# A two-layer diffusion backbone block on one core: 16x16 blocks of the triangular solve inverted on VectorE, another order at the transitions, and the first shift vectors as rows

## What is computed

```
def modulate(h, shift, scale):
    return h * (1.0 + scale) + shift
...
mod = s_lat @ w_ada[l] + b_ada[l]            # s_lat = silu(c); the context has its own vector
...
A = jnp.where(tril_strict, beta[..., :, None] * kk * decay_mat, 0.0)
lhs = A + jnp.eye(C, dtype=F32)
rhs = jnp.concatenate([v * beta[..., None], k * (beta * jnp.exp(G))[..., None]], axis=-1)
sol = lax.linalg.triangular_solve(lhs, rhs, left_side=True, lower=True, unit_diagonal=True)
```

## Time and profile before

| | before |
|---|---|
| median of 3 runs | 2459.61 us (2457.1 to 2466.61) |
| the profiled execution | 2457.2 us, its span 2455.5 us |
| busy, TensorE / VectorE / ScalarE / GpSimd | 2357.0 / 1384.5 / 872.4 / 217.9 us |
| granted clock of TensorE, mean | 0.989 |

### The profile page before, as it was taken

How to read it: one execution, slowest core, us unless ns; L and a number is a source line. 1 busy time by engine, 2 the same in 40 slices (tenths; PEclk the granted TensorE clock), 3 DMA queues, 4 the chain that set the end, 5 groups by cost and what they waited for, 6 DMA issues and landing times. The chain is left out here.

```text
span 2455.5 us, 36528 instructions
## 1 busy us (share of the span) xinstructions
PE 2357.0 (96%) x14022; PEld 2012.8 (82%) x14022; DVE 1384.5 (56%) x2315; ACT 872.4 (36%) x1343; POOL 217.9 (9%) x280
## 2 busy tenths in 40 slices
PE   5999999999999999999999999999999989998998
PEld 5788878886569796888888888888898689888998
DVE  3777875724553435578885255554464543456554
ACT  1533322533441214353322253332255431245553
POOL 3001122000000000211001100000200001001001
PEclk9999999999999999999999999999999999999999
DMA  6455553322020204356554334444334211134555
GB/s 245 134 191 188 192 173 114 130 86 78 32 67 19 78 1 139 115 168 200 188 198 123 95 116 151 148 145 123 94 122 134 65 54 30 47 119 148 182 175 147
DMA packets 96461, 304.05 MB, mean 124 GB/s; under 512 B 10593, under 2 KB 17249, under 8 KB 95329
## 3 DMA queue, kind: packets, MB, share of 16 engines
q1 hardware_dynamic: 76912, 230.87, 29.2%
q0 software_dynamic: 18720, 69.21, 8.6%
q10 hardware_dynamic: 720, 2.44, 0.3%
HBM read 291.99 MB, written 10.49 MB: 123 GB/s over the span
## 5 line engine op out<-in xcount | busy, mean ns | idle before, releaser
L1799 PE MATMUL ps<-h_hi,w_hi 128*128 128x512 f32 (+1 forms) x2176 | 779.5, 358 | 37.2 <-DVE w_lo L1276 26.5
L1801 PE MATMUL ps<-h_hi,w_lo 128*128 128x512 f32 (+1 forms) x2176 | 760.3, 349 | 0.0
L1800 PE MATMUL ps<-h_lo,w_hi 128*128 128x512 f32 (+1 forms) x2176 | 760.2, 349 | 0.0
L1276 DVE TENSOR_TENSOR w_lo<-raw,w_hi 128x1024 fp32r<-128x1024 f32 (+2 forms) x416 | 475.3, 1146 | 470.2 <-ACT w_hi L709 465.9
L709 ACT ACTIVATE w_hi<-raw 128x1024 fp32r<-128x1024 f32 (+2 forms) x416 | 405.2, 975 | 621.7 <-DMA raw<-in_w_down 316.1
L1799 PEld LDWEIGHTS ps<-h_hi,w_hi 128*128 128x128 f32 x2176 | 418.2, 192 | 127.2 <-issue 41.9
L1801 PEld LDWEIGHTS ps<-h_hi,w_lo 128*128 128x128 f32 x2176 | 418.0, 192 | 51.6
L1800 PEld LDWEIGHTS ps<-h_lo,w_hi 128*128 128x128 f32 x2176 | 418.7, 192 | 48.6
L1799 PE MATMUL ps<-a_hi,w_hi 128*128 128x512 f32 (+1 forms) x1050 | 363.0, 346 | 8.3 <-DVE buf_b L1699 3.4
L1801 PE MATMUL ps<-a_hi,w_lo 128*128 128x512 f32 (+1 forms) x1050 | 360.4, 343 | 0.0
L1800 PE MATMUL ps<-a_lo,w_hi 128*128 128x512 f32 (+1 forms) x1050 | 359.0, 342 | 0.0
(11 more groups left out here) (230 smaller groups left out, 1966.5 us busy)
## 6 DMA issues: line engine op xcount, KB each, us to landing
raw<-in_w_up SPq DMA_DIRECT2D x176, 512.0 KB, 3.8
ada<-in_w_ada_t POOLq DMA_DIRECT2D x128, 512.0 KB, 3.9
raw<-in_w_down SPq DMA_DIRECT2D x64, 384.0 KB, 3.2
raw<-in_w_gate SPq DMA_DIRECT2D x48, 512.0 KB, 3.7
raw<-in_w_down SPq DMA_DIRECT2D x64, 320.0 KB, 2.9
raw<-in_w_proj SPq DMA_DIRECT2D x32, 512.0 KB, 3.6
raw<-in_w_merge SPq DMA_DIRECT2D x16, 512.0 KB, 3.9
raw<-in_w_out SPq DMA_DIRECT2D x16, 512.0 KB, 3.5
```

The costliest lines, as they stand in the source:

```text
L1276: vec.tensor_tensor(w_lo[:, j % RING, 0:cols], raw[:, j, 0:cols], w_hi[:, j % RING, 0:cols].bitcast(F32), ALU.subtract).then_inc(s_lo, 1)
L1799: pe.matmul(out, wh, rows_hi[:, i, c], start=first, stop=False)
L1800: pe.matmul(out, wh, rows_lo[:, i, c], start=False, stop=False)
L1801: return pe.matmul(out, wl, rows_hi[:, i, c], start=False, stop=last)
```

## The change

LEVELS begins at 16. `sub_blocks` on VectorE inverts the 16x16 diagonal blocks: it gathers them by 32x32 transposes out of amT into xm, folds the two directions into one triangle, inverts by forward substitution in 28 linked steps, masks, and writes by transposes into tm, which GpSimd has zeroed. Both directions' starting values lie in tm; `t_mat` and `u_mat` name which buffer is T and which U. One set of sixteen transposes gives the other buffer. The prep points get 3 units in place of 4, the Gram products come before the first prep gates, and the lowers of the last finished gate blocks move into the levels. In `split_norm` casts and lowers 0 and 1 come at k = 1 and 3 and the root at k = 7; lag is 3. The first shift vectors are made as rows, [2 x 1024], by 16 matmuls with the conditioning vectors as stationary operand, ahead of the sums; ScalarE copies them out and eight small transposes bring them to columns. w_ada's first part is laid out to suit.

```
-LEVELS = (2, 4, 8, 16, 32, 64)
+LEVELS = (16, 32, 64)
+SUB = LEVELS[0]
+QUAD = 2 * SUB
+PREP_UNITS = 3
...
-        units += [4] * PREP_POINTS + [n - 4 * PREP_POINTS] + list(SCAN_UNITS[l])
+        units += [PREP_UNITS] * PREP_POINTS + [n - PREP_UNITS * PREP_POINTS] + list(SCAN_UNITS[l])
...
-                    for d in range(2):
-                        same = um[:, 8 * d:8 * d + 8, :].rearrange("p q (i c) -> p q i c", c=2)[:, :, :, d]
...
-                    last.then_inc(uid.sem, 1)
+                    pool.memset(tm[:, :, :], 0.0).then_inc(zro.sem, 1)
...
                 if s == 0:
+                    act.wait_ge(s_adad, 1)
+                    act.activation(ada_rows[0:2, :, :], ps[0:2, 2:4, :], ACT.Copy).then_inc(s_adr, 1)
                     casts(0, 2)
...
-                    if k == 2:
+                    if k == 1:
                         weights(0)
+                    if k == 3:
+                        weights(1)
                     if k == 4:
                         last_square(1)
-                        weights(1)
-                    if k == 6:
+                    if k == KD - 1:
                         root(1)
...
+                def sub_blocks(w):
+                    for q in range(P // QUAD):
+                        r = slice(q * QUAD, (q + 1) * QUAD)
+                        last = vec.transpose(sub_raw[r, :].rearrange("p (i t h) -> p i t h", t=16, h=2),
+                                             amT[r, :, r].rearrange("p t (h i) -> p i t h", h=2))
+                    link(last)
...
+                    link(vec.tensor_scalar(sums, raws[:, :, 0, :], half_minus(0), None, ALU.mult))
+                    link(vec.scalar_tensor_tensor(sums, raws[:, :, 1, :], half_minus(1), sums, ALU.mult, ALU.add))
+                    link(vec.tensor_tensor(t, sums, sub_sum.rearrange("p (i j) -> p j i", i=SUB), ALU.add))
+                    link(vec.tensor_copy(sub_t[:, 0:SUB * SUB:SUB + 1], ones[:, 0:SUB]))
+                    for j in range(1, SUB - 1):
+                        size = [P, SUB - 1 - j, j]
+                        part = sub_sum[:, 0:size[1] * j].rearrange("p (i c) -> p i c", c=j)
+                        link(vec.tensor_tensor(part, t[:, j + 1:SUB, j:j + 1].to_broadcast(size),
+                                               t[:, j:j + 1, 0:j].to_broadcast(size), ALU.mult))
+                        link(vec.tensor_tensor(t[:, j + 1:SUB, 0:j], t[:, j + 1:SUB, 0:j], part, ALU.add))
...
+                    vec.wait_ge(edn.sem, edn.at(l, 4 * w + 4))
+                    sub_blocks(w)
...
+                        for n in late[2 * i:2 * i + 1]:
+                            lower(n % RING, b0 + n)
...
-                        if i < 4 and (l == 0 or i % 2 == 0):
-                            decay_queries(w, i)
+                        for n in late[2 * i + 1:2 * i + 2]:
+                            lower(n % RING, b0 + n)
+                        for j in ((0, 1), (2, 3), ())[i]:
+                            if l == 0 or j % 2 == 0:
+                                decay_queries(w, j)
...
+            def first_shifts():
+                pe.wait_ge(s_cact, 1)
                 for k in range(KD):
+                    if k % (ADA_FIRST // 4) == 0:
+                        pe.wait_ge(s_first[k // (ADA_FIRST // 4)], 16)
+                    for m in range(2):
+                        ins = pe.matmul(ps[0:2, 2 + m, :], c_act[:, k, :], ada_first[:, k, m * TOK:(m + 1) * TOK],
+                                        start=(k == 0), stop=(k == KD - 1))
...
-                lag = 2
+                lag = 3
...
-                        if p == 0 and k == 4:
+                        if p == 0 and k == 5:
                             part_sums(s, 1)
...
+                    pe.wait_ge(low.sem, low.at(l, w + 1))
...
+                            elif d:
+                                for j in range(2):
+                                    for q in range(8):
+                                        ins = pe.transpose(ps[:, 2 + 2 * j + q // 4, (q % 4) * P:(q % 4 + 1) * P],
+                                                           tm[:, 8 * j + q, :], ident)
+                                    ins.then_inc(tr0.sem, 1)
+                                pe.wait_ge(tr0e.sem, tr0e.at(l, 2 * w + 2))
+                            columns(i, d)
```

More of the change, by code:

```diff
@@ L1602, in mixer_vec @@
                     gates(delta_point(l, w, PREP_POINTS))
+                    vec.wait_ge(edn.sem, edn.at(l, 4 * w + 4))
+                    sub_blocks(w)
+                    late = [GATE_BLOCK + g + 3 for g in gates_finished(l, delta_point(l, w, PREP_POINTS))]
+                    assert len(late) <= 3
                     for i, b in enumerate(LEVELS):
@@ L2135, in mixer_pe, with columns @@
                     pe.wait_ge(rowd.sem, rowd.at(l, 4 * w + 4))
-                    for d in range(2):
-                        pe.wait_ge(u1.sem, u1.at(l, 2 * w + d + 1))
+                    pe.wait_ge(low.sem, low.at(l, w + 1))
+                    def columns(i, d):
+                        b = LEVELS[i]
                         for q in range(8):
-                            ins = pe.transpose(ps[:, 2 + 2 * d + q // 4, (q % 4) * P:(q % 4 + 1) * P],
-                                               um[:, 8 * d + q, :], ident)
-                        ins.then_inc(tr0.sem, 1)
+                            t = t_mat(d)[:, q, :].rearrange("p (i c) -> p i c", c=2 * b)[:, :, b * d:b * (d + 1)]
+                            ins = pe.matmul(ps[:, d, q * HD:(q + 1) * HD].rearrange("p (i c) -> p i c", c=b),
+                                            amT[:, 8 * d + q, :], t, start=True, stop=True)
+                        ins.then_inc(xps.sem, 1)
@@ L2316, in constants @@
     c[:, C_TRI + P:C_TRI + 2 * P] = i[:, None] >= i[None, :]
-    c[even, C_M1 + even + 1] = -1.0
-    c[even + 1, C_M1 + P + even] = -1.0
+    for h in range(2):
+        c[:, C_HALF + h] = -1.0 * (i % 2 == h)
+    s = np.arange(SUB)
+    low = (i[:, None, None, None] % 2 == np.arange(2)[None, None, :, None]) & (s[None, None, None, :] >= s[None, :, None, None])
+    c[:, C_LOW:C_HALF] = low.reshape(P, -1)
     c[:, C_MIN:C_MIN + P] = np.where(i[:, None] <= i[None, :], 0.0, NEVER)
@@ L2357, in lay_out @@
     out["cT"] = np.stack([v["c"][0], v["c_ctx"]], 1).reshape(KD, P, 2).transpose(1, 0, 2)
-    out["w_ada"] = blocks(v["w_ada"][0][:, :KD * P])
+    out["w_ada"] = v["w_ada"][0][:, :KD * P].reshape(KD, P, KD * P)
     out["w_ada_t"] = v["w_ada"].transpose(0, 2, 1).reshape(DEPTH * ADA, P, D)[KD:]
```

133 lines of the change are left out of this document (67 added, 66 removed).

## The result

The changed kernel takes 2401.98 us in the median of four runs (2394.06 to 2405.19), the kernel before 2460.75 (2457.1 to 2466.61): ratio 0.9745, 95% interval 0.9717 to 0.9774, so it is faster: by 59 us between the medians, by some 63 by the ratio (56 to 70 with its interval). The experiments' gains against the kernel before go by their ratios. The forecast was 2354 and its range ended at 2386: right sign, but a gain of 105 us was forecast and 63 came. Ratios are of executions in the usual state, and one of run 6's four (3713.43 us, at a granted clock of 0.553) is left out of them.

What follows compares the result with a forecast made beforehand. The prediction took TensorE, busy 2357.0 us or 96% of the span, as the bound. Gains of 80 (solve), 13 (transitions) and 12 (start), 105 us in all, from 2457.2 gave 2352, stated as 2354, range 2337 to 2386.

Steps and rivals of the forecast that it cites:

- Levels removed, 107.8 us: Triangular solve: levels 2, 4 and 8 go, 8.98 us each in four solves, 107.8 us off TensorE, all counting.
- I charge 2.5 twice: 5 us: Solves of layer 1: TensorE idles some 12 us and restarts at a low clock, charged 2.5 us twice.
- Rival B: Clock stays low in the start's shift products (15 us lost) and all four solve restarts (5 us): 2374 us; chance 0.10.
- I take 0.70 each: VectorE's block in the solve: eight transposes at 0.70 us, 5.6 in all, within a block of 14.4 us.
- rival D: Solve's strided transposes move element by element; at 5 us each the kernel is slower, 2492 us; chance 0.03.
- VectorE's arrival: Solve: VectorE is ready to start its block 23.9 us after the stage's start in layer 0.
- The order after the wait: Solve's first level: first L2161 comes 6.9 us after the wait, against 5.8 before; delay called 1.2 us with a hop.
- The transitions, 13 us: Four transitions: earlier casts and lowers shorten TensorE's waits for w_lo; 13 us booked, bounds 3 and 17.
- With idle pieces under 2 us I expect it high: Transitions: TensorE's clock stays high, gaining 4.8 us where it had stayed at 0.66.
- Rival C: Transitions give nothing, as the late h_lo takes the place of w_lo: 2364 us; chance 0.10.
- The start, 12 us: Start: 16 products of 512 columns replace 64 small ones for the first shifts, ending at 41 us; gain 12 us.
- A: VectorE's block in the solve is dearer, 20 us, with transposes at twice the price: 2376 us; chance 0.16.

Runs made afterwards that it cites:

- run 6: Changed kernel with the block's eight strided 32-partition transposes replaced by gathering copies and two transposes of 128 partitions: 2397.56 us.
- run 4: Changed kernel with unneeded identity products ahead of TensorE's wait for the blocks, 30 in layer 0 and 70 in layer 1: 2395.5 us.
- run 7: Changed kernel with 33 and 66 unneeded products ahead of the block waits and six in the gap inside the first level: 2377.63 us.
- run 10: Changed kernel again without an edit, for a second profile: median 2401.21 us.
- run 5: Changed kernel with nine more dependent VectorE instructions behind the last block, to price transposes and views: one execution, 2391.9 us.
- run 12: run 11 with 4, 5 and 7 unneeded products ahead of the three waits of each transition: 2360.59 us.
- run 2: Kernel before with the change to the four transitions alone: ratio 0.9959, 10 us faster.
- run 11: run 8 with five more unneeded products ahead of the last solve's wait: 2359.08 us.
- run 9: Kernel before with 21 unneeded dependent VectorE passes in layer 0 ahead of the solve's last starting matrix, making TensorE wait: 2494.68 us.
- run 8: Changed kernel with 128-partition block transposes, unneeded products ahead of block waits (20 and 56), in the gap (six) and in the start: 2366.06 us.

## Why the prediction was wrong

It missed by 41.6 us against the profiled execution, and by 48 against the median. Of the 41.6, 34.2 are the solves', 4.8 the transitions', 1.9 the start's and 0.7 the rest's. By its own steps:

- **Levels removed, 107.8 us**: right. Of the three levels left in each solve the second takes 8.97 us at full clock (756.62 to 765.59), as each of the six did before; the first takes 12.19 with what moved into it, which the sum had as a delay.
- **"I charge 2.5 twice: 5 us"**: this step failed, and it is the largest, 16.6 us in the profiled execution (21.6 less 5) and 21.7 in the second profile. The clock was charged for the long waits of layer 1 alone; for layer 0, with a wait that I put at 2 us, nothing was booked. Runs 4, 6 and 7 show that this is wrong twice over. The stretch behind a wait of 4.3 us loses no less than the one behind 13.6, and the gap of 1.15 us inside the first level, which the change itself brings (the copies that direction 1 waits for), brings the clock down in three of four solves where the wait is filled (14.4 us). Where the gap is filled too, 1.6 us are lost in one solve, behind the 1.79 us of wait that were left, and nothing in the others. Wait and gap together cost 2.5 to 9.8 us in each solve. Rival B named the cause and its sign, but priced it at 2.5 per solve too, by the one row that had it, and put 15 of its 20 us in the start, where they were not lost. The Trainium skill, TensorE: Matmul & The Clock Gate, Part 1, warns that a kernel's slow products differ in number from run to run, and run 10 bears that out; it calls this under 1% of a typical span and advises against fitting it. Here 21.6 to 26.7 us are 0.9 to 1.1% of the span, but the largest part of what is missing from a gain of 4%.
- **"I take 0.70 each"**: the transposes were mis-sized, 1.05; with the closing pass, 1.01, the blocks take 17.8 to 18.0 us and not 14.4, 13.9 in all four. (The terms of the sum came to 14.6; 14.4 was used.) The bounds (11.5 to 20) held it, and both halves of the argument have something in them: 0.70 is the price of a transpose (run 5), and strides do make it dearer, by half and not by the factor of seven that rival D wanted. The row that I used against D, passes through strided views of tm, spoke of views with runs of 2 to 64 neighbours. The small steps (6.6 against 6.7) were right.
- **VectorE's arrival**: it began the block 24.6 and 24.9 us after a stage's start in layer 0 (23.9 forecast) and 20.9 and 19.1 in layer 1 (18.5). With what else is left in the solves this makes 3.7 us.
- **The order after the wait** ("6.9 us", then the rest): right. At full clock the first level takes 12.19 us; the prediction's terms make 12.26 (6.9 to the update's products, then what a level of 8.98 has behind its first 3.62), and ScalarE's copy is waited for as forecast.
- **The transitions, 13 us**: 8.2, within the bounds of 3 to 17. The waits are 0.35, 0.89 and 1.43 us in the first, 2.67 in all where 1.7 were forecast and 4.34 stood before. "With idle pieces under 2 us I expect it high" failed: the clock was 0.90 in three and 0.82 in the second, which lost all it had gained. Run 12 shows that the gaps have to do with it: with them filled it is 1.00 in all four. But in the fourth transition of run 2 and the first of run 11 it was 1.00 with the gaps unfilled (15.2 us each), so the gaps don't bring it down every time. Rival C did not come true.
- **The start, 12 us**: 12.3 at the first product, by a path that was faster than thought (the shifts ended at 38.0 and not 41) into a later wait. 2 us were lost by the first transition, to a longer wait for h_lo (2.13 us and not 1.13 and 0.27) and a second stretch at the low clock (0.62 over 66 to 70 us). These 1.9 us are the start's part of the miss.
- **The rivals and the range.** A (the block at 20) and B (clock) were each priced alone, at 2376 and 2374; both came true in part at once, B in the solves. The range took in A with C, but not A with B.

## What to carry to other kernels

A wait that a change puts on TensorE costs more than its length: here 2.4 and 6.7 us of clock behind a wait alone (run 9), 2.5 to 9.8 with a gap of 1.1 us behind it, and no less behind a wait of 4 us than behind one of 14. So four new waits cost 69 us with their clock (46.9 and 21.6) against the 108 that the removed levels brought. Price it like that from the start, look for the gaps of about 1 us as well (run 4's three cost 14.4 us), and if the wait can't be covered by real products, cover it with idle ones into a free PSUM bank: 222 of them, which compute nothing, made this kernel 24 us faster (run 7). Price a VectorE instruction by the innermost step of its views, and ask of each 32-partition instruction whether one of 128 does the same for the same price.

## What was not expected of the hardware

- A gap of 1.15 us in otherwise full work was followed by some 10 us at 1.2 GHz, 4.8 us of loss, in three of four places (run 4), once with no other gap near it; with the gap filled it stayed at 2.4 GHz in three of four, and the fourth lost 1.6 us behind a wait of 1.79 (run 7). The Trainium skill, TensorE: Matmul & The Clock Gate, in its section on a second failure mode, tells of such small idle pieces between groups of products; these runs agree.
- The same program with the same waits, to 0.02 us, had a stretch of 32.8 us in one execution and 38.2 in another (run 10).
- In the start of the kernel before, the first products of 512 columns went 0.43 us apart while the page's clock says 1.00: pace and granted clock don't always agree, and the pace is the safer reading.
- A VectorE transpose of 128x512 takes 0.71 us, one of 32x512 0.70; a copy of 512 elements 0.43 where a product takes 0.69 (run 5).
- Open: what makes the clock fall at one gap and not at the next like it (1.10 us ahead of a level cost nothing in run 7, 1.14 us cost 1.6 in run 8). The runs show how often and how dear, not why.
